# A dense gated feed-forward on one core: seven block products for eight in the down projection, with gate and up results in one PSUM bank

## What is computed

```python
h = rms_norm(x, ffn_norm_g[l]) * (1.0 + scale_f) + shift_f
y = (silu(h @ w_gate) * (h @ w_up)) @ w_down      # hidden width 2816
x = x + gate_f * y
```

## Time and profile before

| | |
|---|---|
| median of three runs | 2496.72 us (2496.67 to 2498.78) |
| span of the profiled execution | 2499.3 us; a time of its own is not given beside it |
| TensorE busy | 2440.1 us, 98% |
| VectorE busy | 651.3 us, 26% |
| ScalarE busy | 418.3 us, 17% |
| moved by DMA | 617.33 MB |
| 3072 KB weight load, issue to landing | 9.7 to 16.0 us, median 14.5 |

### The profile page before, as it was taken

The page is one execution under the profiler, slowest core; times in us unless marked ns, Lnnn a source line. Parts: engine busy times, 40 slices in busy tenths (PEclk is TensorE's granted clock), DMA queues, the critical chain, the costliest instruction groups (busy, mean ns, idle before and its releaser), DMA issues.

```text
span 2499.3 us, 27928 instructions
## 1 busy us (share of the span) xinstructions
PE 2440.1 (98%) x11210; PEld 1540.3 (62%) x11211; DVE 651.3 (26%) x1441; ACT 418.3 (17%) x1052; POOL 53.8 (2%) x110
## 2 busy tenths in 40 slices
PE   9999999999999999999999999988999989999998
PEld 6666466656565566676777756547996544445444
DVE  0453210011543134455244362101002101011101
ACT  1243010010441132211113112101001101010101
POOL 0000000000000000000000000000000000000000
PEclk9999999999999999999999999998999999999999
DMA  6323344334232688444667458998567999779971
GB/s 263 122 102 126 109 169 168 140 119 157 102 113 106 241 304 312 184 157 169 249 286 303 158 220 362 426 425 368 219 277 300 427 426 426 317 303 425 426 293 80
DMA packets 78971, 617.33 MB, mean 247 GB/s; under 512 B 5984, under 2 KB 6112, under 8 KB 39184
## 3 DMA queue, kind: packets, MB, share of 16 engines
q1 hardware_dynamic: 73920, 558.39, 56.0%
q0 software_dynamic: 4656, 56.47, 5.8%
q10 hardware_dynamic: 288, 0.90, 0.1%
HBM read 614.69 MB, written 1.05 MB: 246 GB/s over the span
## 4 chain that ended last, share of the span: by engine, by line
PE 91%; DMA 5%; DVE 2%; issue 1%; POOL 0%; ACT 0%; SPq 0%; DVEq 0%; POOLq 0%; ACTq 0%
PE G L2160 9%; PE S L2485 8%; PE S L2487 8%; PE G L1883 6%; PE G L1925 5%; DMA big<-in_moe_pack 4%; PE S L2153 4%; PE T L2153 4%; PE G L2501 4%; PE G L2499 4%; PE G L2107 3%; PE S L2371 3%; PE T L2371 3%; PE G L2394 3%; PE S L2553 2%; PE G L2223 2%
## 5 line engine op out<-in xcount | busy, mean ns | idle before, releaser
L2485 PE MATMUL S<-big,hT 128*64 128x256 f32 x2240 | 270.7, 384 | 27.2 <-DMA big<-in_moe_pack 25.6
L2485 PEld LDWEIGHTS S<-big,hT 128*64 128x64 f32 x2240 | 158.4, 137 | 136.6 <-issue 54.3
L2160 PE MATMUL G<-big 128*128 128x512 f32 x512 | 222.2, 592 | 0.0
L1781 DVE TENSOR_TENSOR probs<-S,probs 128x128 f32<-128x128 f32 (+2 forms) x105 | 35.5, 338 | 680.3 <-ACT probs L1100 680.1
L2487 PE MATMUL S<-big,hT 128*128 128x512 f32 x448 | 201.3, 593 | 2.1 <-issue 2.1
L1925 PE MATMUL G<-big,hT 128*128 128x384 f32 x512 | 171.0, 488 | 0.0
L2160 PEld LDWEIGHTS G<-big 128*128 128x128 f32 x512 | 97.2, 190 | 116.0 <-issue 115.3
L1883 PE MATMUL G<-big,hT 128*128 128x372 f32 x512 | 160.8, 476 | 0.4 <-DMA big<-in_proj_pack 0.4
L2487 PEld LDWEIGHTS S<-big,hT 128*128 128x128 f32 x448 | 82.8, 190 | 96.5 <-issue 96.5
L1883 PEld LDWEIGHTS G<-big,hT 128*128 128x128 f32 x512 | 97.0, 190 | 63.4 <-DMA big<-in_proj_pack 1.0
L1925 PEld LDWEIGHTS G<-big,hT 128*128 128x128 f32 x512 | 95.8, 190 | 65.3 <-issue 4.0
(11 more groups left out here) (363 smaller groups left out, 2735.2 us busy)
## 6 DMA issues: line engine op xcount, KB each, us to landing
big<-in_moe_pack SPq DMA_DIRECT2D x112, 2048.0 KB, 15.7
big<-in_moe_pack SPq DMA_DIRECT2D x112, 1024.0 KB, 17.5
big<-in_w_ff SPq DMA_DIRECT2D x32, 2048.0 KB, 8.5
big<-in_ada_pack POOLq DMA_DIRECT2D x24, 2048.0 KB, 14.1
big<-in_ffn_pack SPq DMA_DIRECT2D x11, 3072.0 KB, 14.5
big<-in_gate_pack SPq DMA_DIRECT2D x16, 1536.0 KB, 6.3
big<-in_proj_pack SPq DMA_DIRECT2D x15, 1488.0 KB, 6.2
big<-in_branch_heads SPq DMA_DIRECT2D x6, 2048.0 KB, 7.9
```

The lines of the kernel that those rows point to most:

```text
L2160: return mm(G[j][:, :], hid[:, c % 2, f, b * P:(b + 1) * P], w[:, f, half * 512:(half + 1) * 512], start=(c == 0 and f == 0), stop=(c == 7 ...
L2485: ins = mm(S[s % 2][f * FEW:(f + 1) * FEW, 0:SEQ], hTe[:, k, 0:FEW], wt[:, k, f * SEQ:(f + 1) * SEQ], start=(k == 0), stop=(k == KD - 1))
```

## The change

The output's two token blocks by two halves of 512 columns, and the step's two halves f, make a product of 2 by 2 blocks. It is done with seven block products in place of eight, from sums of blocks. `step_sums(n)` on VectorE forms four sums of the hidden states (`fs1` to `fs4`, 128 columns each), multiplies the gate row into the step's down weights where they lie (2048 columns), and forms four sums of these weights (512 columns each). It waits for the products of step n - 1, whose operands it overwrites. The seven products accumulate over the steps in seven banks `P7`; at the end VectorE joins them into x. The seven banks and the one left over, T0, are all of PSUM, so from step 1 on gate and up of one half share T0 (`ffn_bank`), and a half's products wait until the half before has been read. The sigmoid waits for both gate and up. TensorE's order is written out anew: half 0 of step n, products 1, 2, 3, 5 of step n - 1, half 1 of step n, products 7, 6, 4 of step n - 1, then `down_mm`. The program text of the SP queue and of POOL is not changed. The step counter in place of `x_fin` on VectorE (not shown) changes a semaphore only.

```diff
@@ -95,2 +95,4 @@
 BY_ROWS = QUARTERS[1]
+PRODUCTS = (1, 2, 3, 5, 7, 6, 4)
+LAST_PRODUCTS = (1, 2, 6, 5, 3, 7, 4)
 ROW_L1 = 2 * KD + KCQ + KCKV
@@ -267,2 +269,5 @@
         ffhid = pT[:, :, :].rearrange("p i (f s) -> p i f s", f=FT)
+        f_t1, f_t2, f_t4, fu2, fu3 = (arena[:, i:i + 512] for i in (1024, 1536, 2048, 3072, 3584))
+        f_sum = arena[:, 2560:3072].rearrange("p (i s) -> p i s", i=4)
+        fs1, fs2, fs3, fs4 = (f_sum[:, i] for i in range(4))
@@ -303,2 +308,3 @@
         H4 = [S[0], S[1], T[0], T[1]]
+        P7 = {1: G[0], 2: T[1], 3: S[1], 4: S[0], 5: G[3], 6: G[1], 7: G[2]}
         SCAT = [T[1], G[3], G[0], G[1]]
@@ -373,2 +378,3 @@
         ff2_mm = sig("ff2_mm", 3)
+        sums_ok = sig("sums_ok")
@@ -464,2 +470,10 @@
+        def summed2(n, name):
+            return 0 + 9 * n + ("s3", "s1", "s2", "s4", "wg", "t1", "t3", "t2", "t4").index(name) + 1
+        def ffn_bank(n, f, piece):
+            return H4[2 * f + piece][:, 0:SEQ] if n == 0 else T[0][:, piece * SEQ:(piece + 1) * SEQ]
         def gate_banks(part):
@@ -1070,4 +1084,4 @@
                         act.wait_ge(fhid_ok.sem, n * FT + (f + 1))
-                        act.wait_ge(fg_mm.sem, n * FT + (f + 1))
-                        act.activation(ffsg[:, f, :], H4[2 * f][:, 0:SEQ], ACT.Sigmoid).then_inc(fsg_ok.sem, 1)
+                        act.wait_ge((fu_mm if n else fg_mm).sem, n * FT + (f + 1))
+                        act.activation(ffsg[:, f, :], ffn_bank(n, f, 0), ACT.Sigmoid).then_inc(fsg_ok.sem, 1)
@@ -1679,6 +1692,33 @@
                         dve.wait_ge(fsg_ok.sem, n * FT + (f + 1))
-                        dve.tensor_tensor(ffsg[:, f, :], H4[2 * f][:, 0:SEQ], ffsg[:, f, :], ALU.mult).then_inc(ft_ok.sem, 1)
+                        dve.tensor_tensor(ffsg[:, f, :], ffn_bank(n, f, 0), ffsg[:, f, :], ALU.mult).then_inc(ft_ok.sem, 1)
                         dve.wait_ge(fu_mm.sem, n * FT + (f + 1))
                         dve.wait_ge(ft_ok.sem, n * FT + (f + 1))
-                        dve.tensor_tensor(ffhid[:, i, f, :], H4[2 * f + 1][:, 0:SEQ], ffsg[:, f, :], ALU.mult).then_inc(fhid_ok.sem, 1)
+                        dve.tensor_tensor(ffhid[:, i, f, :], ffn_bank(n, f, 1), ffsg[:, f, :], ALU.mult).then_inc(fhid_ok.sem, 1)
+                def step_sums(n):
+                    h = ffhid[:, n % 2]
+                    a11, a12, a21, a22 = h[:, 0, 0:P], h[:, 1, 0:P], h[:, 0, P:], h[:, 1, P:]
+                    w = ffn_slot((n + 1) % 2)[1]
+                    w11, w12, w21, w22 = w[:, 0, 0:512], w[:, 0, 512:], w[:, 1, 0:512], w[:, 1, 512:]
+                    dve.wait_ge(fhid_ok.sem, (n + 1) * FT + FT)
+                    if n:
+                        dve.wait_ge(down_mm.sem, n)
+                    dve.tensor_tensor(fs3, a11, a21, ALU.subtract).then_inc(sums_ok.sem, 1)
+                    dve.tensor_tensor(fs1, a21, a22, ALU.add).then_inc(sums_ok.sem, 1)
+                    dve.wait_ge(sums_ok.sem, summed2(n, "s1"))
+                    dve.tensor_tensor(fs2, fs1, a11, ALU.subtract).then_inc(sums_ok.sem, 1)
+                    dve.wait_ge(sums_ok.sem, summed2(n, "s2"))
+                    dve.tensor_tensor(fs4, a12, fs2, ALU.subtract).then_inc(sums_ok.sem, 1)
+                    if n == 0:
+                        dve.wait_ge(gateB_ok.sem, gateB_ok.at(l, 4))
+                    dve.wait_ge(arrived_in[(n + 1) % 2].sem, (n // 2 + 1) * 16)
+                    dve.tensor_tensor(w, w, bcast(gateB[1].unsqueeze(1), [P, FT, D]), ALU.mult).then_inc(sums_ok.sem, 1)
+                    dve.wait_ge(sums_ok.sem, summed2(n, "wg"))
+                    dve.tensor_tensor(f_t1, w12, w11, ALU.subtract).then_inc(sums_ok.sem, 1)
+                    dve.wait_ge(sums_ok.sem, summed2(n, "t1"))
+                    dve.tensor_tensor(w12, w22, w12, ALU.subtract).then_inc(sums_ok.sem, 1)
+                    dve.tensor_tensor(f_t2, w22, f_t1, ALU.subtract).then_inc(sums_ok.sem, 1)
+                    dve.wait_ge(sums_ok.sem, summed2(n, "t2"))
+                    dve.tensor_tensor(f_t4, w21, f_t2, ALU.subtract).then_inc(sums_ok.sem, 1)
@@ -1687,2 +1727,3 @@
                         hidden(n, n % 2)
+                        step_sums(n)
                         for c in ADA_SLOTS[1][n]:
@@ -1691,13 +1732,37 @@
                     modulations(l + 1, 1)
-                    dve.wait_ge(gateB_ok.sem, gateB_ok.at(l, 4))
                     dve.wait_ge(mulc_ok.sem, mulc_ok.at(l + 1, 2))
                     dve.wait_ge(x_new.sem, added(u + 1))
-                    for i, j in enumerate(BY_ROWS):
-                        if i < 3:
-                            dve.wait_ge(ff2_mm.sem, ff2_mm.at(DEPTH, i + 1))
-                        else:
+                    def done(i):
+                        if i == LAST_PRODUCTS[-1]:
                             dve.wait_ge(down_mm.sem, FSTEPS)
-                        gated_quarter(j, 1)
-                        if i == 2:
-                            normalise(u + 2, 0)
+                        else:
+                            dve.wait_ge(ff2_mm.sem, ff2_mm.at(DEPTH, LAST_PRODUCTS.index(i) + 1))
+                    def grow(half, b, src):
+                        xs = x[:, b, half * 512:(half + 1) * 512]
+                        return dve.tensor_tensor(xs, src, xs, ALU.add)
+                    done(1)
+                    step.did(dve.tensor_copy(fu2, P7[1][:, :]))
+                    step.do(grow(0, 0, P7[1][:, :]))
+                    done(2)
+                    grow(0, 0, P7[2][:, :]).then_inc(x_new.sem, 1)
+                    done(6)
+                    step.do(dve.tensor_tensor(fu2, P7[6][:, :], fu2, ALU.add))
+                    step.do(grow(1, 0, fu2))
+                    done(5)
+                    step.do(grow(1, 0, P7[5][:, :]))
+                    done(3)
+                    grow(1, 0, P7[3][:, :]).then_inc(x_new.sem, 1)
+                    done(7)
+                    step.do(dve.tensor_tensor(fu3, P7[7][:, :], fu2, ALU.add))
+                    step.did(grow(0, 1, fu3))
+                    step.do(grow(1, 1, fu3))
+                    grow(1, 1, P7[5][:, :]).then_inc(x_new.sem, 1)
+                    normalise(u + 2, 0)
+                    done(4)
+                    grow(0, 1, P7[4][:, :]).then_inc(x_new.sem, 1)
                 else:
@@ -2370,49 +2435,43 @@
                     for k in range(KD):
-                        ins = mm(H4[2 * f + piece][:, c0:c1], w[:, k, f * SEQ + piece * P:f * SEQ + (piece + 1) * P], hT[:, k, c0:c1], start=(k == 0), stop=(k == KD - 1))
+                        ins = mm(ffn_bank(n, f, piece)[:, c0:c1], w[:, k, f * SEQ + piece * P:f * SEQ + (piece + 1) * P], hT[:, k, c0:c1], start=(k == 0), stop=(k == KD - 1))
                     return ins
-                def up_step(n):
+                def first_step():
-                    pe.wait_ge(arrived_in[(n + 1) % 2].sem, (n // 2 + 1) * 16)
-                    if n == 0:
-                        for piece in range(2):
-                            for f in range(FT):
-                                pe.wait_ge(fhid_ok.sem, f + 1)
-                                up_piece2(n, piece, f, 0, P)
-                            if piece == 0:
-                                second_block()
-                        second_ready()
+                    pe.wait_ge(arrived_in[1].sem, 16)
+                    for piece in range(2):
+                        for f in range(FT):
+                            pe.wait_ge(fhid_ok.sem, f + 1)
+                            up_piece2(0, piece, f, 0, P)
+                        if piece == 0:
+                            second_block()
+                    second_ready()
                     for piece in range(2):
                         for f in range(FT):
-                            pe.wait_ge(fhid_ok.sem, n * FT + (f + 1))
-                            up_piece2(n, piece, f, P if n == 0 else 0, SEQ).then_inc((fg_mm, fu_mm)[piece].sem, 1)
+                            up_piece2(0, piece, f, P, SEQ).then_inc((fg_mm, fu_mm)[piece].sem, 1)
-                def down_piece(n, f, j):
+                def down_product(n, i):
-                    half, b = divmod(j, 2)
-                    dn = ffn_slot((n + 1) % 2)[1]
-                    return mm(G[j][:, :], ffhid[:, n % 2, f, b * P:(b + 1) * P], dn[:, f, half * 512:(half + 1) * 512],
-                              start=(n == 0 and f == 0), stop=(n == FSTEPS - 1 and f == FT - 1))
+                    h = ffhid[:, n % 2]
+                    w = ffn_slot((n + 1) % 2)[1]
+                    left = {1: h[:, 0, 0:P], 2: h[:, 1, 0:P], 3: fs4, 4: h[:, 1, P:], 5: fs1, 6: fs2, 7: fs3}[i]
+                    right = {1: w[:, 0, 0:512], 2: w[:, 1, 0:512], 3: w[:, 1, 512:], 4: f_t4, 5: f_t1, 6: f_t2, 7: w[:, 0, 512:]}[i]
+                    pe.wait_ge(sums_ok.sem, summed2(n, {1: "wg", 2: "wg", 3: "wg", 4: "t4", 5: "t1", 6: "t2", 7: "t3"}[i]))
```

(52 more changed lines are left out.)

## The result

The changed kernel takes 2631.0 us (median of four runs, 2625.2 to 2634.3) where the kernel before takes 2497.4 (2496.7 to 2498.8): 1.053 times as long, 95% interval 1.0517 to 1.0547. Forecast were 2606 us and a range of 2583 to 2630. The profiled execution has a span of 2632.5 us, 133.2 more than the 2499.3 of before.

The account below looks back on a forecast made before the run. TensorE, busy for 98% of the span, was taken to bound the kernel. Terms of -9.4 + 90.9 + 22.0 + 0 + 6.3 = +109.8 us on 2496.7 gave 2606 us, with a range of 2583 to 2630.

Parts of the forecast that it names:

- Down products: TensorE in the stage: seven products for eight in each of 11 steps, 176 records become 154, 9.4 us less.
- Nine waits for weights: Before steps 2 to 10 TensorE waits 10.1 us for a load whose cover is gone: +90.9 us, bounds 87 to 147.
- the modulation loads would keep clear: Modulation loads no longer start together with the weight loads, so a landing takes the quiet 9.8 us.
- The clock: TensorE's clock drops in each of nine idle times, 2.45 us each to regain: +22.0 us, bounds 0 to 53.
- VectorE beside the waits: VectorE's added sums and multiplications, 6.2 us a step, and modulation work are hidden by the waits for weights: 0.
- the third rival: Load hidden, but VectorE's modulation work stands before the next hidden state: 40.5 us, kernel at 2534 us; chance 0.02.
- First hand-over: Step 1 waits for the bank step 0 still holds, +0.5 us; the gap before the last products goes, -0.5.
- The end: Stage end: TensorE idles 3.5 us for scaled weights, 0.25 for a sum, 2.6 before turning: +6.3 us.
- The differences carry over: Closing step: the sum of +109.8 us is added to the runs' median of 2496.7 us, giving 2606 us.
- the clock fell: Against a rival where idle times of 10 us leave TensorE's clock alone: 22 us off, 2584; that rival's chance 0.05.
- the loads did not crowd: Against a rival where modulation loads meet weight loads in eight steps: +44 us, 2650; that rival's chance 0.07.

Follow-up runs that it names:

- run 4: The kernel before the change, eight down products kept, with each weight load of steps 2 to 9 sent one step late: 2632.3 us (1.054).
- run 2: The changed kernel with 38 short products of no use on TensorE in each of the nine waits for weights: 2602.9 us (1.041).
- run 1: The changed kernel with each step's weights in two loads, gate and up columns sent earlier, down rows as before: 2574.5 us (1.031).
- run 3: The changed kernel with eleven short products of padding in the first wait for weights, nothing else: 2615.4 us (1.046).
- run 9: The changed kernel with split load, modulation chunks between the halves, gate row early and a plain last step of eight products, no padding: 2494.0 us (0.9979).

## Why the prediction was wrong

Its steps, against the trace:

- **Down products**, -9.4: 154 records, a pair still 0.86 us. Right.
- **Nine waits for weights**, +90.9: 93.0, between 9.8 and 11.8 each. Right; the first landed in 11.7 us, not 9.8. That the modulation loads would keep clear was right too, and run 4 shows what it was worth (13.5 to 15.3 us a wait where they don't).
- **The clock**, +22.0: the first 32 records after the waits sum to 86.4 us where nine times 6.91 is 62.2: +24.2. Right, and run 2 takes most of it away. The example of the Trainium skill ("TensorE: Matmul & The Clock Gate", section "HAM oscillation — how this bites in real kernels") would have given 7.5 us; this trace has 2.0 to 3.3 us a restart, and run 2 took 2.5 a restart away.
- **VectorE beside the waits**, 0: right. Passes of 0.29, 2.28 and 0.69 us, as taken from the line. That the waits were the cover was right as well: run 1 took them away and 40.9 us of the third rival appeared.
- **First hand-over**, 0: right, 0.6 us for the forecast 0.5, and the 0.5 before the last products is gone.
- **The end**, +6.3: 11.5. The waits are 3.5 and 3.7 us, as forecast in kind, but the clock falls around both, which the sum had left out. The seven last products take 7.9 us (1505.6 to 1513.5) and not 6.0, and the turning and gate products after the second wait end 2.4 us late (1517.19 to 1541.13 against 1400.42 to 1422.00):

```profile
1506.00:1510.00 4.00, 4.00 (x7) 1.58 (x7) 3.83 (x10) 0.00 (x0) 0.52 (x1) 0.64 0.01 2
...
1517.00:1521.00 4.00, 3.81 (x11) 2.77 (x12) 2.10 (x6) 2.54 (x6) 0.04 (x1) 0.50 1.01 430
```

So the stage with its first turnings costs +119.1 where +109.8 was forecast. That alone would have given 2616, inside the range.

**The step that failed** is the one after the sum: "The differences carry over: 2496.7 + 109.8". It took the 1100 us behind the stage as untouched, because no instruction in them is changed. They cost 14.1 us more (133.2 - 119.1), because the code ahead of the experts is eleven products shorter. In the trace the two gaps are 12.0 us longer and the groups behind them 5.2 us slower, 17.1 together; 3.1 us came back elsewhere, above all in a group of 16 records that took 12.06 us before, at a clock of 0.69, and 8.50 now, at 0.99 (12.19 in run 3, so it isn't the edit). Run 3 takes the gaps away and lands at 2615.4, inside the range; 11.7 us of its gain lie behind the stage. The row that could have warned is the earlier trace rows: an idle time of 6.75 us ended by "issue", with no producer late. I used it for the clock and never asked what it was.

The place of the forecast among its rivals was right, then: the clock fell, the loads did not crowd, VectorE was late only where the wait had gone. Its range had no room for a cost outside the stage.

The end, sized at 6.3 and measured at 11.5, is the second largest miss; waits and clock add 2.1 and 2.2.

What stays open: which instruction's place decides (one product separates -11 from -10, and run 9 differs from the changed kernel in its waits as well), what the 7 us between the last product and the next are made of, and why the second gap of 3 us sits at another group.

## What to carry to other kernels

Before work is put behind the products of the next step, look at the signal that frees the buffer: moved by one step it uncovers the whole transfer, here nine times 10 us for 9 us of products. Splitting the transfer by who reads which part gave the cover back, but the saving only showed after the queue that the wait had been hiding, and then the end of the stage, were put right as well. And where a program branches beside heavy transfers, a few instructions more or less ahead of the branch are a variable: try the kernel with some padding before a difference of half a per cent is put down to the edit.

## What was not expected of the hardware

An edit moved idle time into code 700 us behind its stage in which nothing had changed: 14 us by eleven products fewer in TensorE's program, gone with eleven of padding, back with 64 more. A packet of instructions (0.02 MB) comes in among weight loads at a DMA share of 1.0 with and without a gap, 4 us behind the last product; with a gap of 7 us a second one follows 6 us later. One such gap is in every kernel of this case, the first one included. It also costs clock: the 16 records after it took 10.1 and 9.3 us in place of 7.1. And 38 short products in a wait of 10 us were worth 2.5 us in seven waits of nine, since they kept the clock at 1.00; where they ended 2.3 to 2.5 us before the weights came, the clock fell two times in four (8.86 us for 32 records).
